# Strassen's method for a layer's up projection: seven products of 128 token columns, with the weight sums on VectorE

## What is computed

```python
h = _rmsnorm(x, norm_ffn[l]) * (1 + sc_f) + sh_f
u = _causal_dwconv(h @ ffn_w_up[l], ffn_conv_w[l], ffn_conv_b[l])
ua, uv = jnp.split(u, 2, axis=-1)
x = x + g_f * ((jax.nn.silu(ua) * uv) @ ffn_w_down[l])
```

## Time and profile before

| | us |
|---|---|
| median of 3 runs | 1915.2 (1913.84 to 1915.67) |
| profiled execution, its span | 1916.5 |
| TensorE busy | 1862.5 (97%) |
| VectorE busy | 632.3 (33%) |
| ScalarE busy | 416.8 (22%) |
| up projection, layer 0 and layer 1 | 152.0 each |

### The profile page before, as it was taken

How to read it: one execution, slowest core, us unless ns; L and a number is a source line. 1 busy time by engine, 2 the same in 40 slices (tenths; PEclk the granted TensorE clock), 3 DMA queues, 4 the chain that set the end, 5 groups by cost and what they waited for, 6 DMA issues and landing times.

```text
span 1916.5 us, 20449 instructions
## 1 busy us (share of the span) xinstructions
PE 1862.5 (97%) x8734; PEld 1301.3 (68%) x8734; DVE 632.3 (33%) x1155; ACT 416.8 (22%) x886; POOL 0.8 (0%) x9
## 2 busy tenths in 40 slices
PE   6999999999999999999999999999999999999997
PEld 3477787888888758678888888865764434434432
DVE  4452266432223335227642222034441111111112
ACT  4253122212210234312212121012421111111112
POOL 0000000000000000000000000000000000000000
PEclk9999999999999999999999999999999999999999
DMA  9753363364536665337245443463429999999993
GB/s 388 262 181 129 132 219 134 131 220 143 165 136 230 220 247 176 132 120 274 89 164 188 146 162 138 144 219 132 155 89 429 427 428 428 427 428 428 427 427 140
DMA packets 137434, 443.27 MB, mean 231 GB/s; under 512 B 8832, under 2 KB 58240, under 8 KB 123520
## 3 DMA queue, kind: packets, MB, share of 16 engines
q1 hardware_dynamic: 134912, 438.26, 60.4%
q10 hardware_dynamic: 2432, 3.71, 0.6%
HBM read 440.12 MB, written 1.84 MB: 231 GB/s over the span
## 4 chain that ended last, share of the span: by engine, by line
PE 90%; DVE 4%; DMA 2%; ACT 2%; DVEq 1%; issue 1%; PEldq 0%; SPq 0%; ACTq 0%; PEld 0%
PE acc L713 36%; PE acc L1185 12%; PE acc L723 7%; PE aux L1224 6%; PE aux L1014 4%; PE acc L1014 4%; PE acc L1172 3%; PE acc L1036 3%; PE aux L644 2%; PE acc L1233 2%; PE aux L1233 2%; DMA ring<-in_ada_first 1%; PE acc L989 1%; PE aux L658 1%; DMA ring<-in_w_in 1%; PE acc L1129 1%
## 5 line engine op out<-in xcount | busy, mean ns | idle before, releaser
L713 PE MATMUL acc<-hT,ring 128*128 128x256 f32 x2688 | 588.3, 380 | 1.0 <-ACT hT L1383 1.0
L713 PEld LDWEIGHTS acc<-hT,ring 128*128 128x128 f32 x2688 | 509.0, 190 | 76.9 <-issue 8.5
L1185 PE MATMUL acc<-ring,yT 128*64 128x512 f32 x512 | 169.2, 594 | 0.0
L723 PE MATMUL acc<-ring,hT 128*128 128x512 f32 (+1 forms) x352 | 148.8, 581 | 3.4 <-DMA ring<-in_w_in 2.9
L2148 DVE SCALAR_TENSOR_TENSOR area<-acc,vectors,area 128x255 f32<-128x255 f32 (+1 forms) x176 | 72.7, 475 | 208.7 <-ACT area L1560 207.1
L723 PEld LDWEIGHTS acc<-ring,hT 128*128 128x128 f32 x352 | 66.2, 190 | 79.4 <-issue 75.5
L2393 DVE TENSOR_TENSOR xT<-xT,acc 128x1024 f32<-128x1024 f32 x17 | 20.8, 1221 | 290.3 <-PE acc L1233 290.3
L1762 DVE SCALAR_TENSOR_TENSOR ring<-ring,cspread 128x1024 f32<-128x1024 f32 x80 | 93.1, 1220 | 64.4 <-DMA ring<-in_ada_rest 64.4
L1185 PE MATMUL acc<-area,yT 128*64 128x512 f32 x384 | 112.9, 593 | 0.0
L1185 PEld LDWEIGHTS acc<-ring,yT 128*64 128x64 f32 x512 | 52.4, 137 | 74.5 <-issue 74.5
L1310 ACT ACTIVATE area<-aux 128x512 f32<-128x512 f32 (+3 forms) x65 | 41.7, 675 | 236.3 <-PE aux L644 230.7
(11 more groups left out here) (392 smaller groups left out, 2005.4 us busy)
## 6 DMA issues: line engine op xcount, KB each, us to landing
ring<-in_w_in SPq DMA_DIRECT2D x34, 2048.0 KB, 9.9
ring<-in_ffn_w_up SPq DMA_DIRECT2D x44, 1024.0 KB, 7.7
ring<-in_ada_rest SPq DMA_DIRECT2D x20, 2048.0 KB, 8.0
ring<-in_w_up SPq DMA_DIRECT2D x17, 2048.0 KB, 18.8
ring<-in_w_down SPq DMA_DIRECT2D x17, 2048.0 KB, 18.4
ring<-in_w_gate SPq DMA_DIRECT2D x16, 2048.0 KB, 15.6
area<-in_w_up SPq DMA_DIRECT2D x12, 2048.0 KB, 19.2
area<-in_w_down SPq DMA_DIRECT2D x12, 2048.0 KB, 17.8
```

The lines of the kernel that those rows point to most:

```text
L713: mm = pe.matmul(acc[LU.buf[use]][:, SEQ * j:SEQ * j + SEQ], w[:, k, c0:c0 + P], x[:, k, :], start=(k == 0), stop=(k == n - 1))
L723: mm = pe.matmul(acc[LU.buf[use]][:, at:at + width], x[:, k, P * t:P * t + P], w[:, k, :], start=(k == 0), stop=(k == n - 1))
L1185: mm = pe.matmul(dst[CAP * e:CAP * e + CAP, :], xg[:, b, k, CAP * e:CAP * e + CAP], w[:, k, :], start=(k == 0), stop=(k == KT - 1))
```

## The change

A chunk's product C = W x H is cut in two along each side: W into a11, a12 (gate half, features 0-511 and 512-1023 of the input), a21, a22 (value half), H into b11, b12 (the first 512 input features, tokens 0-127 and 128-255), b21, b22. Seven products of (2 x 128 outputs) x (512 inputs) x (128 tokens) take the place of eight. A product (`up_product`) is 8 matmuls with 128 moving columns; a chunk has 56 matmuls.

The four weight sums (s1, s2, s4 and a11 - a21, which overwrites a21) are tensor_tensor instructions of DVE over 128 x 1024 elements, for each chunk. Four sums of `hT` (`tsum`, 128 x 512 each) are made once a layer, in the memory of `zb`. Five of the products add up in one 256-column region of `acc[b]` ("main"), out of which ACT copies four intermediate results into `c4` (in SBUF); one product goes to a second region of `acc[b]`, and one region of `aux2` or `pmod` ("fifth") takes two. DVE adds the second and fifth regions onto `c4`. The taps are then computed from `c4`. Some semaphores elsewhere are merged under new names (`mid_n`, `mid_rt`, `router_full`, ...), in the same places. The chunk's slot is released after its fifth count of `acc_full` instead of the fourth.

```diff
-              ... [(f"up{i}", 4) for i in range(11)] + [("dn0", 0)]
+              ... [(f"up{i}", 5) for i in range(11)] + [("dn0", 0)]
...
+        s1, s2, s4 = (view(10752 + 1024 * i, 4, 256) for i in range(3))
+        c4 = shaped(gates[:, 1].rearrange("p k n -> p (k n)"), 2, 4, SEQ)
+        tsum = shaped(zb.rearrange("p t n -> p (t n)"), 4, 4, P)
...
+        def up_regions(i):
+            b = LU.buf[f"up{i}"]
+            return acc[b][:, 0:SEQ], acc[b][:, 512:512 + SEQ], (aux2, pmod)[b][:, 0:SEQ]
...
PE
+                def up_product(dst, w, x, signal, opens=False, fresh=None):
+                    for k in range(4):
+                        if fresh is not None:
+                            pe.wait_ge(h_ready, fresh + k + 1)
+                        for j in range(2):
+                            mm = pe.matmul(dst[:, P * j:P * j + P], w[:, k, P * j:P * j + P], x[:, k, :],
+                                           start=(opens and k == 0 and j == 0), stop=(k == 3), skip_group_check=True)
+                    mm.then_inc(signal, 1)
+                def up_first(i):
+                    arrived(f"up{i}")
+                    open_acc(f"up{i}")
+                    up_product(main, a11, b11, acc_full[b], True, ...)
+                def up_next(i):
+                    up_product(second, a12, b21, up_second, True, ...)
+                def up_middle(i):
+                    pe.wait_ge(s_ready, 3 * n + 2)
+                    pe.wait_ge(t_ready, 4 * l + 2)
+                    pe.wait_ge(first_out, n + 1)
+                    up_product(main, s2, tsum[:, 1], acc_full[b])
+                    up_product(fifth, s1, tsum[:, 0], up_fifth, True)
+                    pe.wait_ge(s_ready, 3 * n + 3)
+                    pe.wait_ge(t_ready, 4 * l + 3)
+                    pe.wait_ge(main_out, 3 * n + 1)
+                    up_product(main, a21, tsum[:, 2], acc_full[b])
+                def up_last(i):
+                    pe.wait_ge(t_ready, 4 * l + 4)
+                    pe.wait_ge(main_out, 3 * n + 2)
+                    up_product(main, a22, tsum[:, 3], acc_full[b])
+                    pe.wait_ge(s4_ready, n + 1)
+                    pe.wait_ge(fifth_out, n + 1)
+                    up_product(fifth, s4, b22, acc_full[b])
+                up_first(0)
+                up_next(0)
+                up_first(1)
                 for i in range(11):
-                    gate_pieces(f"up{i}", 0, 4, fresh=2 * KT * l + KT if i == 0 else None)
+                    up_middle(i)
+                    if 0 < i < 10:
+                        up_first(i + 1)
+                    if i < 10:
+                        up_next(i + 1)
+                    up_last(i)
...
ACT
+                def up_copy(i, piece, signal):
+                    full(f"up{i}", piece)
+                    v, t = ((0, 0), (0, 1), (1, 1), (1, 0))[piece]
+                    copy(c4[:, i % 2, 2 * v:2 * v + 2, P * t:P * t + P], shaped(up_regions(i)[0], 2, P)).then_inc(signal, 1)
+                def up_first_taps(i):
+                    act.drain()
+                    act.wait_ge(c_done, 11 * l + i + 1)
                     for j in range(4):
-                        act.activation(u4[:, i % 2, j, :], full(f"up{i}", j | 1)[:, SEQ * j:SEQ * j + SEQ], ACT.Identity, ...
+                        act.activation(u4[:, i % 2, j, :], c4[:, i % 2, j, :], ACT.Identity, ...
+                up_copy(0, 0, first_out)
+                up_copy(1, 0, first_out)
+                for i in range(12):
+                    if i:
+                        up_first_taps(i - 1)
+                    if i < 11:
+                        up_copy(i, 1, main_out)
+                        up_copy(i, 2, main_out)
+                    if i:
+                        freed(f"up{i - 1}")
+                        act.activation(sl[:, (i - 1) % 2, :], ..., ACT.Silu).then_inc(u_silu, 1)
+                    if 0 < i < 10:
+                        up_copy(i + 1, 0, first_out)
+                    if i < 11:
+                        up_copy(i, 3, main_out)
...
DVE
+                def up_sums(i):
+                    dve.wait_ge(landed[slot], value)
+                    if i:
+                        dve.wait_ge(up_fifth, 11 * l + i)
+                    tt(s1, a21, a22, ALU.add).then_inc(s_ready, 1)
+                    D_()
+                    tt(s2, s1, a11, ALU.subtract).then_inc(s_ready, 1)
+                def up_difference(i):
+                    tt(a21, a11, a21, ALU.subtract).then_inc(s_ready, 1)
+                def up_fourth(i):
+                    D_()
+                    if i:
+                        dve.wait_ge(*up_spent(l, i - 1))
+                    tt(s4, a12, s2, ALU.subtract).then_inc(s4_ready, 1)
                 for i in range(2):
                     for j in (0, 2):
                         add_to_x(full(f"wo{i}", j + 1), j, 4 * i + j, gmh)
                     D_().then_inc(*free(f"wo{i}"))
                     if i == 0:
+                        up_sums(0)
+                        up_difference(0)
+                        up_fourth(0)
...
+                tt(tsum[:, 0], b12, b11, ALU.subtract).then_inc(t_ready, 1)
...
+                def up_taps(i):
                     dve.wait_ge(u_tap, 44 * l + 4 * i + 4)
                     for k in (1, 0):
                         for j in range(4):
-                            last = stt(u4[..., d:], acc[...][...], ..., u4[..., d:], ALU.mult, ALU.add)
+                            last = stt(u4[..., d:], c4[:, i % 2, j, 0:SEQ - d], ..., u4[..., d:], ALU.mult, ALU.add)
                     last.then_inc(*free(f"up{i}"))
+                up_take_second(0)
+                for i in range(11):
+                    if i:
+                        up_taps(i - 1)
+                    dve.wait_ge(main_out, 3 * n + 2)
+                    dve.wait_ge(up_fifth, n + 1)
+                    up_add(i, 1, 1, 2).then_inc(fifth_out, 1)
+                    if i < 10:
+                        up_sums(i + 1)
+                        up_take_second(i + 1)
+                        up_difference(i + 1)
+                    if i:
+                        up_gate(i - 1)
+                    dve.wait_ge(*up_spent(l, i))
+                    up_add(i, 0, 1, 2).then_inc(c_done, 1)
+                    if i < 10:
+                        up_fourth(i + 1)
+                up_taps(10)
+                up_gate(10)
```

More of the change, by code:

```diff
@@ L193 @@
               ("xbc0", 4), ("xbc1", 4), ("xbc2", 4), ("xbc3", 4), ("bb0", 4), ("bb1", 4), ("gc0", 4), ("gc1", 4),
-              ("bc0", 4), ("bc1", 4), ("wo0", 4), ("wo1", 4)] + [(f"up{i}", 4) for i in range(11)] + [("dn0", 0)]
+              ("bc0", 4), ("bc1", 4), ("wo0", 4), ("wo1", 4)] + [(f"up{i}", 5) for i in range(11)] + [("dn0", 0)]
 assert len(LAYER_USES) % 2 == 0
@@ L469, in program @@
         u_tap, u_silu, act_ready = (sem(n) for n in ("u_tap", "u_silu", "act_ready"))
[L471 to L476, removed]
+        s_ready, s4_ready, t_ready = (sem(n) for n in ("s_ready", "s4_ready", "t_ready"))
+        up_second, up_fifth, first_out, main_out, fifth_out, c_done = (
+            sem(n) for n in ("up_second", "up_fifth", "first_out", "main_out", "fifth_out", "c_done"))
+        late_in, mid_n, t2, t2_out = (sem(n) for n in ("late_in", "mid_n", "t2", "t2_out"))
+        a2_ss, mid_rt = sem("a2_ss"), sem("mid_rt")
+        on_full, oT_t, oT_out = (sem(n) for n in ("on_full", "oT_t", "oT_out"))
+        router_full, router_sub, router_exp = sem("router_full"), sem("router_sub"), sem("router_exp")
+        og_ready, routed = sem("og_ready"), sem("routed")
         pm_ready, gx_full, gx_out, pt_full, pt_out = (sem(n) for n in ("pm_ready", "gx_full", "gx_out", "pt_full", "pt_out"))
@@ L485, in program, with up_quarters, up_spent @@
         block = ctx.enter_context(nc.Block())
+        def up_regions(i):
+            b = LU.buf[f"up{i}"]
+            return acc[b][:, 0:SEQ], acc[b][:, 512:512 + SEQ], (aux2, pmod)[b][:, 0:SEQ]
+        def up_quarters(slot):
+            w = shaped(ring[:, slot, :], KT, 2, 256)
+            return w[:, 0:4, 0], w[:, 4:8, 0], w[:, 0:4, 1], w[:, 4:8, 1]
+        def up_spent(l, i):
+            b = LU.buf[f"up{i}"]
+            return acc_full[b], l * LU.per_full[b] + LU.full[f"up{i}"] + 5
         def release_of(l, name):
@@ L1155, in _ @@
                     keep_busy(2, aux2[:, 0:256])
-                    pe.wait_ge(h2_out, t)
-                transposes([(hT[:, k, P * t:P * t + P], aux[:, P * k:P * k + P]) for k in range(KT)], h2_t)
+                    pe.wait_ge(tok_out, T + t)
+                transposes([(hT[:, k, P * t:P * t + P], aux[:, P * k:P * k + P]) for k in range(KT)], tok_t)
             keep_busy(1, aux2[:, 0:256])
@@ L1634, in _ @@
             for t in range(T):
[L1635 to L1640, removed]
+                act.wait_ge(tok_t, T + t + 1)
+                copy(shaped(h2t[:, t, :], KT, P), aux.rearrange("p (m k) -> p k m", k=KT)).then_inc(tok_out, 1)
```

(8 more changed lines are left out.)

98 lines of the change are left out of this document (67 added, 31 removed).

## The result

| | before | after |
|---|---|---|
| median of runs | 1915.13 us (1913.84 to 1915.67, 4 runs) | 1904.24 us (1903.11 to 1907.36, 4 runs) |
| ratio, with 95% interval | | 0.9944 (0.9931 to 0.9956) |
| profiled execution: span | 1916.5 us | 1904.4 us |
| loop of the up projection, each layer | 152.0 us | 147.75 us |

The change is faster by 10.9 us, inside the range of the prediction (1889 to 1913), and above the 0.2% that a measurement of this kernel can tell. The forecast was 14.6. The profiled execution of the changed kernel is its slowest run, 1907.36 us, around a span of 1904.4.

A forecast was written before the change was run, and what follows sets the result against it. The prediction took PE as the bound: a layer's loop 137.9 of records + 5.8 of stalls + 0.96 in the last chunk = 144.7 us against 152.0, twice 7.3 less, giving 1900.6 us, range 1889 to 1913.

The forecast's parts named there:

- What bounds the kernel: Whole run: PE is busy for 97% of the span, so a microsecond taken out of the loop comes out of the run.
- PE's work: Up-projection loop: 112 records a chunk at 0.112 us, 12.54 us a chunk, 1.27 us less than before.
- Rival D: Up-projection matmuls: weight loads stand exposed at 0.19 us a record, a chunk takes 21.3 us, result 2080; chance 0.01.
- DVE's work: Up-projection loop: sums, taps, adds and gate product take 10.5 us a chunk, fitting into 12.54 with 2 us to spare.
- Rival C: Weight sums on DVE: reading the ring with gaps makes DVE the bound, at twice the price about 1939 us; chance 0.06.
- The chain that binds: Before `up_first`: add, ACT's taps and DVE's taps take 6.01 us against three products' 5.37, stalling PE 0.64 us, nine times a layer.
- ACT's four taps: Chain ahead of `up_first`: four taps from SBUF, priced like L1383, spaced 0.40 with 0.49 for the last, 1.69 us.
- One margin: End of a chunk: PE wants `fifth_out` only after ten more microseconds.
- The sum: Each layer's loop: 137.9 + 5.8 + 0.96 = 144.7 us against 152.0, 7.3 less, twice 14.6.
- Ends and neighbours: Around the loops: first chunk's sums hidden, ending some 0.5 us ahead of the next add; layer 1's transfer holds by 0.4 us.
- Rival A: Up-projection loop: the chain fits under the three products, no stall, 138.9 us a layer, result 1889; chance 0.10.
- Rival B: Chain ahead of `up_first`: hand-overs and instructions do not overlap; from 6.83 us the gain is gone, result 1908 to 1921; chance 0.12.

The follow-up runs named there:

- e11: The kernel before, with each up piece computed for 128 tokens after the other (eight narrow products, no sums): 1927.59 us, ratio 1.0059.
- e1: The changed kernel, with PE opening the buffer from chunk 2 on after the last add onto `c4` and ACT's fourth copy: 1884.34 us, loop 138.45 us.
- e6: e1 with two more DVE instructions of 1024 columns a round, results unused: 1903.04 us, loops 144.5 us.
- e3: The changed kernel with one more DVE instruction of 1024 columns a round, result unused: 1906.89 us, loops 148.2 and 148.5 us.
- e10: The kernel before with four more DVE instructions of 1024 columns a round, results unused: 1915.11 us, ratio 0.9995.
- e5: The changed kernel, with DVE waiting for ACT's first taps one by one instead of for all four: 1888.30 us, loop 139.50 us.
- e2: The changed kernel with ACT's first tap lacking its scale operand, bias kept: 1896.45 us, loops 144.4 us.
- e12: The changed kernel with ACT's first tap lacking its bias operand, scale kept: 1899.26 us, loops 144.4 us.

## Why the prediction was right, and where it was off

- **What bounds the kernel.** Right. The loop was PE's, and what it lost came out of the run.
- **PE's work.** Right: 0.1117 us a record against 0.112, in the change and in e11. Rival D is out: weight loads of 0.19 us follow one another every 0.1117 us, (1.87 - 0.19) / 15 in the row above, and in e1 PE is busy for 137.87 of 138.43 us. The Trainium skill (TensorE: Matmul & The Clock Gate, Part 3, "The mechanism") says that weight loads overlap matmuls in flight only when the row group differs; for these full tiles the trace disagrees. I had read it one-sidedly: the same section also lets a load run ahead when it goes to the background weight buffer, which no run here can tell apart.
- **DVE's work.** Right in size (103.7 us busy a loop, "some 100") and in its slack: 10.76 us a round in e1's trace, and 13.01 - 2.27 = 10.74 by e6, against 10.5. Rival C is out: the sums that read the ring with gaps last 1.22 us, as long as the row without gaps, and e3, e6 and e10 agree.
- **The chain that binds.** Right in mechanism and place, shown by e1 and e5; one term was mis-sized. "ACT's four taps ... 1.69" measured 2.08 us. I had taken the row of L1383, which has a bias and no scale, for an instruction with both. The nearer row was L1560, with both operands, though from PSUM: two in 1.02 us, spaced some 0.46; with that spacing and 0.56 for the last the four come to 1.95. e2 and e12 show what the wrong row left out: the second operand. The add took 0.42 instead of 0.48, the taps 3.41 instead of 3.38. The stall was 1.03 instead of 0.64, nine times a layer, twice: 7 us. One margin was misread without harm: `fifth_out` is ready at 492.17 and PE wants it at 497.59, 5.4 us later and not ten.
- **The sum.** 144.7 us a loop against 147.75: 3.5 by the stall, less 0.3 by the spacing of the records and 0.2 by the last chunk, where ACT's copy took 0.39 and not 0.56. The loops alone gave 8.5 us where 14.6 were forecast; that the run gained 10.9 is owed in part to what lies ahead of them, about 2.2 us that the forecast did not hold. In so far the number is better than its working, by luck; with the loops alone the run would stand at 1906.6, still inside the range.
- **Ends and neighbours.** Right: no wait of PE behind `wo1`, at the sums of `hT` or at the down projection shows in the list of waits. With the first chunk's sums in place DVE still idles 0.57 us ahead of the add of `wo1` in both layers (0.5 forecast), and it does not wait for layer 1's transfer.
- **Rival A** (no stall, 138.9 a loop, 1889) is what e1 makes of the kernel, 138.45 and 1884; that it falls below 1889 is in part the transfer. **Rival B** did not come: the chain was 6.4 us, not 6.83. But its answer, that every piece stands in the rows at the lower price, was wrong for ACT's taps, and its upper end put 0.56 on one that lasts 0.59.

## What to carry to other kernels

When work is moved so that a buffer's last reader becomes another instruction, move the count that frees the buffer with it: here that one wait was worth 18.6 us in the two loops, more than the change itself. Take a duration from a row with the same operands, not only the same size: four activations of 256 columns took 2.08 us with bias and scale, and 1.71 with one of them. And a product saved in eight is paid partly in narrower matmuls and partly in the order of the engine that combines the results; add up its chain, not only its busy time.

## What the runs showed of the hardware

- A float32 matmul record of 128 columns is issued every 0.1117 us and one of 256 every 0.216, weight loads of 0.19 us included: halving the columns costs 3.4% more per column (2 x 0.1117 / 0.216; e11 and the kernel before).
- ACT's activations of 256 columns from SBUF with a scale and a bias operand last 0.59 us and start 0.49 apart; with either alone, 0.49 and 0.40 (e2, e12). From PSUM with both operands one lasts 0.56 (L1560 before), and a copy of 256 columns from PSUM 0.38.
- After a wait for DVE's taps PE's next record started 0.14 us after the last tap ended and lasted 0.347 us instead of 0.275.
- The same transfer of 2 MB took 13.2 to 14.4 us from issue to landing in four kernels and 10.4 to 10.7 in ten others, though the matmuls and transfers up to that place are the same; the cause is open.
- In the router's stage the granted clock was 0.50 over a longer stretch in some executions than in others, at the same work, which cost that stage 1.7 us.
